# A three-block network on one core: five residual products joined to the stages behind them, and two row norms taken as one factor

## The reference, cut to what matters

```python
h = h + y @ w_out                          # block 1: mixers, then their output product
h = h + attention(rmsnorm(h, xa_g), ...)   # it ends in  o @ wo
h = h + conv_ffn(rmsnorm(h, ffn_g))
# block 2: mixer, merge of two branches, then
h = h + merged @ w_o
h = h + (relu(rmsnorm(h, norm2_g) @ w_ff_in) ** 2) @ w_ff_out
x = rmsnorm(h, norm_f_g)                   # block 2 ends in a norm
# block 3
h = concat([meta, x])                      # 16 meta rows ahead of the 512
h = h + hybrid_mixer(rms_norm(h, norm_mix_w))
h = h + conv_ffn_3(rms_norm(h, norm_ffn_w))
return rms_norm(h, norm_final_w)[16:]
```

## Time and profile before

| | |
|---|---|
| median of 3 runs | 3016.01 us |
| the profiled execution, its own time | 3011.13 us |
| its span, first to last instruction | 3009.8 us |
| PE busy | 2846.4 us (95%) |
| DVE busy | 1572.8 us (52%) |
| ACT busy | 1056.0 us (35%) |
| POOL busy | 578.9 us (19%) |
| mean granted clock of TensorE | 0.959 |

### The profile page before, as it was taken

How to read it: one execution, slowest core, us unless ns; L and a number is a source line. 1 busy time by engine, 2 the same in 40 slices (tenths; PEclk the granted TensorE clock), 3 DMA queues, 4 the chain that set the end, 5 groups by cost and what they waited for, 6 DMA issues and landing times. The chain is left out here.

```text
span 3009.8 us, 42733 instructions
## 1 busy us (share of the span) xinstructions
PE 2846.4 (95%) x16698; PEld 2393.2 (80%) x16698; DVE 1572.8 (52%) x2429; ACT 1056.0 (35%) x1798; POOL 578.9 (19%) x472
## 2 busy tenths in 40 slices
PE   8989999999999999999999998999898999999998
PEld 6769876778888766757788887976787899999986
DVE  5854556455653464834433336765344435476643
ACT  4353333432222323252423223445344232422233
POOL 2530101121100121440100002045354000111101
PEclk9987899999999999989999999998899899999999
DMA  4200231123232312202222331210000022222221
GB/s 156 89 2 6 75 103 62 43 85 98 91 98 98 109 63 72 84 15 77 84 98 91 98 97 52 92 36 1 6 2 1 32 90 76 85 85 92 92 98 63
DMA packets 60309, 210.63 MB, mean 70 GB/s; under 512 B 7927, under 2 KB 8567, under 8 KB 59991
## 3 DMA queue, kind: packets, MB, share of 16 engines
q1 hardware_dynamic: 59974, 207.46, 20.9%
q10 hardware_dynamic: 144, 0.52, 0.0%
HBM read 205.84 MB, written 2.10 MB: 69 GB/s over the span
## 5 line engine op out<-in xcount | busy, mean ns | idle before, releaser
L272 PE MATMUL ps<-normed_hi,slab_hi 128*128 128x264 f32 (+2 forms) x2568 | 870.5, 339 | 34.4 <-DVE normed_lo L565 15.8
L274 PE MATMUL ps<-normed_hi,slab_lo 128*128 128x264 f32 (+2 forms) x2568 | 854.1, 333 | 0.0
L273 PE MATMUL ps<-normed_lo,slab_hi 128*128 128x264 f32 (+2 forms) x2568 | 854.0, 333 | 0.0
L153 ACT ACTIVATE slab_hi<-ring 128x1024 fp32r<-128x1024 f32 x376 | 397.6, 1058 | 1016.7 <-PE ps L274 998.9
L157 DVE TENSOR_TENSOR slab_lo<-ring,slab_hi 128x1024 fp32r<-128x1024 f32 x360 | 475.9, 1323 | 428.2 <-ACT slab_hi L153 427.4
L272 PEld LDWEIGHTS ps<-normed_hi,slab_hi 128*128 128x128 f32 x2568 | 488.7, 190 | 102.9 <-issue 50.4
L273 PEld LDWEIGHTS ps<-normed_lo,slab_hi 128*128 128x128 f32 x2568 | 488.7, 190 | 51.8 <-issue 4.3
L274 PEld LDWEIGHTS ps<-normed_hi,slab_lo 128*128 128x128 f32 x2568 | 486.8, 190 | 49.9
L273 PE MATMUL ps<-hidden_lo,slab_hi 128*128 128x512 f32 x608 | 238.7, 393 | 0.0
L274 PE MATMUL ps<-hidden_hi,slab_lo 128*128 128x512 f32 x608 | 238.5, 392 | 0.0
L272 PE MATMUL ps<-hidden_hi,slab_hi 128*128 128x512 f32 x608 | 236.6, 389 | 0.0
(11 more groups left out here) (544 smaller groups left out, 3992.2 us busy)
## 6 DMA issues: line engine op xcount, KB each, us to landing
ring<-in_stream SPq DMA_DIRECT2D x376, 512.0 KB, 3.3
h<-in_x SPq DMA_DIRECT2D x8, 256.0 KB, 5.6
mix_y<-in_sgu_b SPq DMA_DIRECT2D x1, 1024.0 KB, 6.0
out_features<-ffn_hidden SPq DMA_DIRECT2D x2, 512.0 KB, 3.1
xn<-in_c_recip_count SPq DMA_DIRECT2D x1, 512.0 KB, 3.2
rwkv_a<-in_mem SPq DMA_DIRECT2D x1, 512.0 KB, 3.9
rwkv_b<-in_mem SPq DMA_DIRECT2D x1, 512.0 KB, 5.0
sgu_ln<-in_sgu_ln SPq DMA_DIRECT2D x1, 512.0 KB, 7.6
```

The lines of the kernel that those rows point to most:

```text
L153: self.nc.scalar.activation(self.hi[:, n % PARTS, :], self.ring[:, n % SLOTS, :], ACT.Copy).then_inc(self.hi_ready, 1)
L272: nc.tensor.matmul(to, lhsT[0], rhs[0], start=start, stop=False)
L273: nc.tensor.matmul(to, lhsT[0], rhs[1], start=False, stop=False)
L274: return nc.tensor.matmul(to, lhsT[1], rhs[0], start=False, stop=stop)
```

## The change

It does five things.

1. The three `residual_stage`s and `residual_3_stage` are no stages of their own: they become `Residual` and `Residual3`, whose lists run ahead of the next stage's within one block (before the cross-attention's queries, the first feed-forward, block 2's feed-forward and block 3's). Their split rows share the buffers of the feed-forward's hidden rows. The first product behind waits for the low rows k-tile by k-tile, and each bank for its own addition (`free`). The squares of the next norm are taken while the banks drain, and `norm_at` is 1 where it was 3.
2. Block 2's feed-forward and the third block's 25 products are one stage with the residual product ahead of them (`Network2`). `norm_stage` goes. The third block's rows are split straight out of `h` with the product of both gains (`CarriedRows`), the 16 meta rows apart by VectorE.
3. Block 2's own norm, which `h` of block 3 needs, is taken behind the products (`LastNorm`): squares on ScalarE at products 2 and 3, 7 additions on GpSimd, sums on TensorE after product 6, a root on ScalarE and its inverse on VectorE at 7 (behind `Rates.sums`), spreads on TensorE after product 8, 8 gained copies on ScalarE, 8 multiplications on GpSimd.
4. The gates of block 3 use a factor in which block 2's norm is divided out (`leave_factor`, VectorE at product 14). The clearing of `fox_v` moves from the stage's start to product 13, GpSimd's clearing of the query buffer behind the 8 multiplications.
5. `merge_stage`'s second group takes its last two steps jointly.

```diff
+class CarriedRows(Rows):
...
+    def split_hi(self, act, k):
+        self.K.nc.scalar.activation(self.hi[:, k, META:T3], self.h[:, k, 0:S], ACT.Copy, scale=self.gains.both[:, k:k + 1]).then_inc(self.hi_ready, 1)
+    def split_lo(self, dve, k):
+        dve.wait_ge(self.hi_ready, k + 1)
+        self.K.nc.vector.scalar_tensor_tensor(out=self.lo[:, k, META:T3], in0=self.h[:, k, 0:S], scalar=self.gains.both[:, k:k + 1],
+                                              in1=self.hi[:, k, META:T3].bitcast(F32), op0=ALU.mult, op1=ALU.subtract).then_inc(self.lo_ready, 1)
+    def take_square(self, act, k):
+        if k >= 2:
+            act.wait_ge(self.added, max(1, k - 2))
+        self.K.nc.scalar.activation(self.square[:, k % 2, META:T3], self.h[:, k, 0:S], ACT.Square, scale=self.gains.weight[:, k:k + 1]).then_inc(self.squared, 1)
...
+    def meta(self, dve, link):
+        nc, gains = self.K.nc, self.gains
+        dve.wait_ge(gains.meta_arrived, 16)
+        hi, lo, total = self.hi[:, :, 0:META], self.lo[:, :, 0:META], self.total[:, 0:META]
+        link(nc.vector.tensor_tensor(gains.gained[:], gains.meta, self.K.vec_all("norm_mix_w_3").unsqueeze(2).to_broadcast((P, KT, META)), ALU.mult))
+        link(nc.vector.tensor_copy(hi, gains.gained[:]))
+        link(nc.vector.tensor_tensor(lo, gains.gained[:], hi.bitcast(F32), ALU.subtract))
+        link(nc.vector.tensor_tensor(gains.gained[:], gains.meta, gains.meta, ALU.mult))
+        link(nc.vector.tensor_reduce(total, gains.gained[:].rearrange("p k t -> p t k"), AX, ALU.add))
+        nc.vector.tensor_scalar(total, total, (EPS - EPS * EPS) * D / P, None, ALU.add).then_inc(self.meta_ready, 1)
+    def sums(self, pe):
+        pe.wait_ge(self.meta_ready, 1)
+        super().sums(pe)
...
+class CarriedGains:
...
+    def vector(self, dve):
+        K, nc = self.K, self.K.nc
+        last = K.vec_all("norm_f_g_2")
+        nc.vector.tensor_tensor(self.both[:], last, K.vec_all("norm_mix_w_3"), ALU.mult).then_inc(self.ready, 1)
+        nc.vector.tensor_tensor(self.weight[:], last, last, ALU.mult).then_inc(self.squared, 1)
+    def scalar(self, act):
+        act.wait_ge(self.squared, 1)
+        act.wait_ge(self.ready, 1)
+        self.K.nc.scalar.activation(self.weight[:], self.weight[:], ACT.Sqrt, bias=self.K.eps_col).then_inc(self.ready, 1)
+        act.dma_start(self.meta, self.ins["meta"]).then_inc(self.meta_arrived, 16)
...
+class LastNorm:
+    def __init__(self, K, ctx, rows, factor):
+        self.K, self.h, self.to, self.rows, self.factor = K, K.h, K.xn, rows, factor
+        self.total = rows.total[:, META:T3]
...
+    def squares(self, act, tiles):
+        for k in tiles:
+            self.K.nc.scalar.activation(self.to[:, k, META:T3], self.h[:, k, 0:S], ACT.Square).then_inc(self.squared, 1)
+    def add(self, pool):
+        pool.wait_ge(self.rows.summed, 1)
+        for k in range(1, KT):
+            pool.wait_ge(self.squared, k + 1)
+            if k > 1:
+                pool.wait_ge(self.added, k - 1)
+            self.K.nc.gpsimd.tensor_tensor(self.total, self.to[:, 0, META:T3] if k == 1 else self.total, self.to[:, k, META:T3], ALU.add).then_inc(self.added, 1)
+    def sums(self, pe):
+        pe.wait_ge(self.rows.scaled, 1)
+        pe.wait_ge(self.added, KT - 1)
+        for i in range(4):
+            last = self.K.nc.tensor.matmul(self.K.ps[:, 6, i:i + 1], self.total[:, i * P:(i + 1) * P], self.K.ones[:, 0:1], start=True, stop=True)
+        last.then_inc(self.summed, 1)
+    def root(self, act):
+        act.wait_ge(self.summed, 1)
+        self.K.nc.scalar.activation(self.rstd[:], self.K.ps[:, 6, 0:4], ACT.Sqrt, bias=self.K.eps_col, scale=1.0 / D).then_inc(self.rooted, 1)
+    def invert(self, dve):
+        dve.wait_ge(self.rooted, 1)
+        self.K.nc.vector.reciprocal(self.rstd[:], self.rstd[:]).then_inc(self.inverted, 1)
+    def spreads(self, pe):
+        pe.wait_ge(self.inverted, 1)
+        for i in range(4):
+            last = self.K.nc.tensor.matmul(self.K.ps[:, 7, i * P:(i + 1) * P], self.rstd[:, i:i + 1].to_broadcast((P, P)), self.K.ident, start=True, stop=True)
+        last.then_inc(self.spread, 1)
+    def keep(self, act):
+        act.wait_ge(self.spread, 1)
+        self.K.nc.scalar.activation(self.scale, self.K.ps[:, 7, :], ACT.Copy).then_inc(self.kept, 1)
+    def gain(self, act, tiles):
+        act.wait_ge(self.added, KT - 1)
+        for k in tiles:
+            self.K.nc.scalar.activation(self.to[:, k, META:T3], self.h[:, k, 0:S], ACT.Copy, scale=self.K.vec("norm_f_g_2", k)).then_inc(self.gained, 1)
+    def norm(self, pool):
+        pool.wait_ge(self.kept, 1)
+        for k in range(KT):
+            pool.wait_ge(self.gained, k + 1)
+            self.K.nc.gpsimd.tensor_tensor(self.to[:, k, META:T3], self.to[:, k, META:T3], self.scale, ALU.mult).then_inc(self.normed, 1)
+    def leave_factor(self, dve, link):
+        dve.wait_ge(self.normed, KT)
+        link(self.K.nc.vector.reciprocal(self.scale, self.scale))
+        self.K.nc.vector.tensor_tensor(self.scale, self.scale, self.rows.scale[:, META:T3], ALU.mult)
+        self.K.nc.vector.tensor_copy(self.factor[:, 0:META], self.rows.scale[:, 0:META])
...
+        if rows.before and i < self.turns:
+            for c in range(len(self.halves)):
+                rows.before.free(pe, (self.first + len(self.halves) * i + c) % self.cut)
         for k in range(KT):
-            if i == 0 and not rows.split:
+            if i == 0 and (rows.before or not rows.split):
...
-        for k in range(KT):
-            rows.take_square(act, k)
-            if k == 3:
-                slabs.hi_upto(act, self.n0 + (2 if rows.split else 3))
+        if not rows.before:
+            for k in range(KT):
+                rows.take_square(act, k)
+                if k == 3:
+                    slabs.hi_upto(act, self.n0 + (2 if rows.split else 3))
...
+            if then.before:
+                if m == KT - 1:
+                    self.slabs.hi_upto(act, self.n0 + self.count + 1)
+                if m:
+                    then.take_square(act, m - 1)
+        if then.before:
+            then.take_square(act, KT - 1)
+    def free(self, pe, b):
+        pe.wait_ge(self.added, self.order.index(b) + 1)
...
+class Residual:
+    def __init__(self, K, rhs, steps, then, parts):
+        self.K, self.then = K, then
+        self.filled, self.added = K.sem("out_filled"), K.sem("h_added")
+        self.feed = Feed(K, None, steps, rhs, [S], parts=PARTS, at=parts)
+        self.group = Group(self.feed, KT, 0, steps, self.filled, joint=True)
+        then.come_from(self)
+    def free(self, pe, b):
+        pe.wait_ge(self.added, b + 1)
...
+    def scalar(self, act):
+        feed, then = self.feed, self.then
+        feed.start_hi(act)
+        feed.ahead_hi(act, self.group.body)
+        for m in range(KT):
+            act.wait_ge(self.added, m + 1)
+            then.split_hi(act, m)
+            if m == KT - 1:
+                feed.slabs.hi_upto(act, feed.n0 + feed.steps + 1)
+            if m:
+                then.take_square(act, m - 1)
+        then.take_square(act, KT - 1)
+    def vector(self, dve):
+        K, feed, then = self.K, self.feed, self.then
+        feed.start_lo(dve)
+        feed.ahead_lo(dve, self.group.body)
+        for m in range(KT):
+            self.group.bank_ready(dve, m)
+            K.nc.vector.tensor_tensor(K.h[:, m, 0:S], K.ps[:, m, :], K.h[:, m, 0:S], ALU.add).then_inc(self.added, 1)
+            if m:
+                then.split_lo(dve, m - 1)
+        then.split_lo(dve, KT - 1)
...
-        groups = [Group(feed, KT, 4 * g, 4, filled, 7 * g) for g in range(2)]
+        groups = [Group(feed, KT, 4 * g, 4, filled, 7 * g, joint=g == 1) for g in range(2)]
...
+class Network2:
+    TILES = FF2 // P
...
+    def scalar(self, act, then):
+        nc, ffn = self.K.nc, self.ffn
+        self.out.scalar(act)
+        self.gains.scalar(act)
+        ffn.start_hi(act)
...
+        ffn.down_hi(act, self.squared)
+        ffn.rows_hi(act, then)
+    def vector(self, dve, then, link):
+        nc, ffn = self.K.nc, self.ffn
+        self.gains.vector(dve)
+        self.out.vector(dve)
+        ffn.start_lo(dve)
...
+        ffn.down_lo(dve)
+        dve.wait_ge(self.gains.ready, 2)
+        then.meta(dve, link)
+        ffn.add_residual(dve, (0, S), then)
...
+                network.sync(sp)
+                K.slabs.refill(sp, cols.n0 + 1, 2)
+                sp.wait_ge(network.ffn.added, KT)
...
+                    pe.wait_ge(last_norm.kept, 1)
...
-                warm(K, 0, 2)
+                network.tensor(pe)
...
+                    if i == SUMS:
+                        last_norm.sums(pe)
+                    if i == SUMS + 2:
+                        last_norm.spreads(pe)
...
+                network.scalar(act, rows)
                 cols.start_hi(act)
                 for i in range(TILES):
                     if NORM <= i < NORM + 8:
```

(32 more changed lines are left out.)

332 lines of the change are left out of this document (167 added, 165 removed).

## The result

The kernel after takes 2996.34 us, the median of nine runs (2978.93 to 3002.65), beside 3016.15 of the kernel before in the same session (nine runs, 3010.34 to 3024.13). The ratio is 0.9934, with the 95% interval 0.9914 to 0.9955: 20 us less, where 30 were forecast. It is inside the range and 10 us above the forecast of 2986.0; a gain of 30 us lies outside the interval, which spans 14 to 26. The profiled executions stand at 3011.13 and 2994.56, 16.6 us apart; by these two traces the sum of the prediction is judged, term by term.

What follows compares the result with a forecast made beforehand. TensorE, busy 2846.4 of 3009.8 us, was taken as the bound. 48.2 us saved less 6.0, 1.7 and 10.5 gave 30.0, so 3016.0 became 2986.0, range 2975 to 3000 (its own 2981 to 2991).

Steps and rivals of the forecast that it cites:

- joins 1 and 2: Residuals joined to cross-attention and to the first feed-forward: the meetings go, 4.2 us and 2.8 us less.
- 660.94: Trace time where TensorE kept its usual pace, read as waits below 1.5 us bringing no slow stretch.
- join 4: Second network into block 3's products: norm stage and slow stretch go, 21.9 us, plus 5.2 for the wait of `sums`.
- The merge: Last two steps taken jointly: 3.8 us won at its end, 1.5 of new wait, net 2.3 us.
- Join 5: Residual joined to block 3's feed-forward: the meeting goes, 4.0 us less.
- (a): Drains at the joins: GpSimd's additions delay VectorE's splits, so TensorE waits for low rows, 6.0 us in all.
- rows 7: Trace rows of VectorE's splits and slab parts beside GpSimd, read as a partial hold of 0.8 us per addition.
- (c): Last norm's spreads after product 8 wait 8.8 us for VectorE's inversion behind `Rates.sums`; with slow stretch, 10.5 us.
- the full hold: Rival: GpSimd holds VectorE fully, joins cost 6 us more, spreads 15.8; 19 us left, 2997; chance 0.15.
- VectorE is not held: Rival: no delay by GpSimd, drains cost 1 us and spreads 6.4; 39 us less, 2977; chance 0.14.
- becomes the bound of the stage: Rival: the last stage waits for VectorE, TensorE losing 31 us there; slower than before at 3023; chance 0.04.
- (d): Work moved to ScalarE, GpSimd, VectorE and DMA in the last stage: put at nothing; uncovered VectorE work would cost 4 us.

Runs made afterwards that it cites:

- e5: The kernel after with three row buffers in block 2's merge instead of two, their address moving from 64 to 192 modulo 256: 2975.99 us, one run.
- e4: The kernel after with the next norm's squares taken behind the residual's drain, in product 0, and not within it: 3020.71 us, one run.
- e2: The kernel after with six of the last norm's seven GpSimd additions cut to 4 columns from 512, leaving its sum incomplete: 2992.97 us, one run.
- e3: The kernel after with the buffers of split rows put at other addresses modulo 256 bytes by small gaps: 2979.33 us, one run.
- e7: e6 with only the slabs (weights) moved from 128 to 0 modulo 256, the moving rows staying at 128: 2991.75 us, one run.
- e8: e7 with the moving rows' address table at 0 instead of 128, so slabs and rows both lie at 0: 2955.66 us, one run.
- e6: The kernel after with e1, e5, split buffers at 128 modulo 256 and block 3's part stride a multiple of 256: 2953.20 us, ratio 0.9809.
- e1: The kernel after with the last norm's inversion ahead of `Rates.sums` and its spreads after product 9 instead of 8: 2988.93 us, ratio 0.9921.

## Why the prediction was right, and where it was too high

**What went, by its own steps.** *Joins.* The meetings went as forecast. The lines of the table for joins 1 and 2 (5.2 for 4.4, 1.0 for 3.4) mislead: each begins with its residual, and the slow stretch of 1.6 us that went from the first to the second lies ahead of both joins. Counted from its residual's last matmul, join 1 paid 3.6 up to the product behind `sums`, and join 2, with the wait of 1.40 gone, 2.6 up to the stage's end; 0.4 of what each lacks is the wait of 1.26, which takes 1.4 from start to start where 1.0 was put. The same wait of 2.51 us had a slow stretch behind it in one kernel and none in the other, so the length of a wait does not settle it; the forecast had put 1 to 2 us for this in its range and nothing in its sum. Nor are waits below 1.5 us safe, as the prediction read from 660.94: in join 4 the slow stretch begins behind one of 1.24. *Join 4*, the largest term, gave what it should: the 20.3 us are gone, with the stage, and the sums' wait of 3.19; its new waits are 0.51 + 0.69 + 1.24 with a slow stretch of 1.6, 4.0 us, where 2.7 were taken and 3.7 was the bound. Of the 6.3 us that lack in that line of the table, 4.2 are pace (below), 1.6 the slow stretch, and 0.5 small things, net of 0.9 that the stretch behind the merge lost less than before. *The merge* gave 2.9 for 2.3, 0.6 of it by a shorter slow stretch; its new wait is 1.54 for 1.5, and e5 shows its cause to be the one told. *Join 5* gave 3.8 for 4.5, with 1.0 lost to the pace.

**What came.** (a) The drains beside GpSimd: 1.26 us at joins 1 to 3 for 1.0. That the additions cause it is shown (e4), but the hold is not partial, as the prediction read rows 7. The addition of 460.65 ends at 462.20, and the slab part that began beside it at 460.97 ends at 463.28, 1.08 later. So it goes throughout the kernel after: of VectorE's instructions with two large inputs in SBUF that begin during one of GpSimd's norm additions, all 13 slab parts end 1.08 to 1.09 us after that addition, all 20 of 512 columns 0.55 after, and all 6 of 528 columns 0.56 or 0.57 after, however early they had begun; the 16 additions out of PSUM keep 0.68 to 0.69. Rows 7 say the same: the two slab parts of 4.61 end 1.08 behind two additions. The Trainium skill, SBUF — State Buffer, section Who interferes with whom, calls the shared ports an exclusive lock, and by it the loser is blocked until the other is done; the trace agrees. What an addition costs is less than its length because VectorE begins partway through it, and works out of PSUM during others: 5.1 us for the seven additions of join 1, 0.73 each where 0.8 was forecast. The size was right by averaging, the mechanism was not.

(c) The spreads: wait 8.33 for 8.8, GpSimd's part 3.3 for 4.0 (e2); the slow stretch 2.5 for 1.6, since it took in the spreads themselves. The line is 1.9 worse than forecast: 1.57 are a slow stretch behind product 3, whose idle grew from 1.44 to 1.87.

*The rivals.* 2996.34 is nearer to the 2997 of the full hold than to the forecast. That rival has the hold right and its price wrong: it charged each addition in full, 13.3 us at the spreads where 8.33 were waited. The rivals in which VectorE is not held, or becomes the bound of the stage, are out: no product from 9 on waits for it. That the time is in the range owes something to the range's width, for it lies outside the 2981 to 2991 that the forecast gave itself.

**What was missing.** Of the 13.4 us between 30.0 and 16.6, 5.2 are a term that the sum did not have. The step that failed is the one that cost the moved buffers at nothing: (d) looked at who works and who waits, not at where the shared buffers come to lie. The residual's and the second network's hidden rows went from 192 to 224 modulo 256, and with the slabs at 128 that is 0.2333 us a matmul for 0.2289: 768 of the network's output products cost 3.4, 182 of the residual 0.8; the last network's output, 527 at 0.2308 for 0.2289, costs 1.0. e3, e7 and e8 show the mechanism, and e6 takes it back with more. Another 3.2 are slow stretches at join 4 and behind product 3, and 0.9 the spreads at the lower clock; 3.1 lie between the fox scores and block 3's residual, of which 2.0 is the clock in the stage that normalises heads (its spreads alone take 7.69 us where they took 6.24), with no instruction of it changed. The rest is small waits, less 1.5 that slow stretches around the merge gave back. These shifts of the clock were seen, not tested.

## What to carry to other kernels

Joining stages pays what the meeting cost, minus what the engine behind it is already late: look in the drain for the engine with no room, and in each engine's list for what stands ahead of a small step that another engine will stop for (here one reciprocal of 0.14 us behind 5.5 us of scans: 9 us with its slow stretch, once the spreads came a product later too). Beside GpSimd, count when a VectorE instruction with two inputs in SBUF begins: it ends behind the addition that it meets. When a change moves buffers, compare the matmul pace of untouched products first, for a fraction of a per cent there outweighs most waits. Where operands can be placed, give weights and moving rows the same address modulo 256 bytes, strides included: here that, with e1's order and three buffers, took the time to 2953, 1.9% below the kernel before.

## What the runs showed of the hardware

**Addresses.** A 512-column matmul chain took 0.2267 us a matmul with both operands alike modulo 256 bytes and up to 0.2343 otherwise, 3.4%, for any of the buffers tried. The Trainium skill, SBUF — State Buffer, section Who interferes with whom, gives the moving operand and the weight load a port each, independent of one another. Taken alone, that gives no reason for the places to matter, and the measurement decides. The 264-column matmuls stayed at 0.1207 to 0.1222 in every kernel; their rows' tiles lie 2112 bytes apart, so that no placing makes all of them alike, and it wasn't tried.

**A stage at one or the other clock.** The time of one kernel varied by some 24 us between executions (the kernel after: 2978.93 to 3002.65). Only one execution of each kernel has a trace, so where they differ is not shown; between kernels it is in one place above all. Windows with TensorE's granted clock (again the last but two column) over the stage of the chunks, kernel after and then e5: the same matmuls run at 2.4 GHz in e5 and at 1.2 after 233 us in the kernel after, which is through the stage 14 us later. What happens ahead of 222 us is alike in both to 0.7 us. What decides it stays open.

```profile
232.00:242.00 10.00, 9.68 (x47) 9.68 (x47) 3.88 (x6) 1.52 (x3) 0.00 (x0) 0.53 0.01 2
```

```profile
232.00:242.00 10.00, 10.00 (x92) 10.00 (x92) 7.85 (x11) 0.85 (x2) 0.00 (x0) 1.00 0.01 2
```
